# A hybrid-attention decoder layer: expert gathers in slots of 128 tokens, one PSUM copy of the tokens for the dot products, and deeper gather rings

## The reference, cut to what matters

```python
q = (xc @ w_pq).reshape(c, 8, 2, 128)                       # 8 heads, two half-queries
s = jnp.einsum('chpd,hpkd->chpk', q, sub_keys)
sv, si = lax.top_k(s, 16)                                   # best 16 keys of each half
cand = (sv[:, :, 0, :, None] + sv[:, :, 1, None, :]).reshape(c, 8, -1)
cid = (si[:, :, 0, :, None] * 128 + si[:, :, 1, None, :]).reshape(c, 8, -1)
cv, ci = lax.top_k(cand, 16)                                # 16 experts a head: 128 a token
eid = jnp.take_along_axis(cid, ci, axis=-1)
gate = jax.nn.softmax(cv, axis=-1)
act = jax.nn.gelu(jnp.einsum('chkd,cd->chk', u_emb[eid], xc), approximate=False)
out = jnp.einsum('chk,chkd->cd', gate * act, v_emb[eid])    # 1024 floats of u and of v an expert
```

## Time and profile before

| | |
|---|---|
| median of three timed runs | 1012.64 us (1012.56 to 1013.12) |
| span of the profiled execution | 1080.4 us |
| DMA moved in the span | 381.54 MB, mean 353 GB/s |
| of it POOL's queue (gathers) / SP's queue | 304.81 MB / 75.78 MB |
| busy: PE / DVE / ACT / POOL | 69% / 64% / 37% / 58% |
| gathers issued by POOL | 576 |

### The profile page before, as it was taken

The page is one execution under the profiler, slowest core; times in us unless marked ns, Lnnn a source line. Parts: engine busy times, 40 slices in busy tenths (PEclk is TensorE's granted clock), DMA queues, the critical chain, the costliest instruction groups (busy, mean ns, idle before and its releaser), DMA issues.

```text
span 1080.4 us, 13828 instructions
## 1 busy us (share of the span) xinstructions
PE 742.8 (69%) x4217; PEld 379.1 (35%) x4217; DVE 686.7 (64%) x1725; ACT 404.0 (37%) x1154; POOL 622.1 (58%) x584
## 2 busy tenths in 40 slices
PE   8999986554798677766536768757637567765444
PEld 3575834111354435543212233323213235231111
DVE  1363776997288543698695559988974535639542
ACT  1162142332356470333223346354516742322412
POOL 0000275777667765475565656766775665667664
PEclk9999997877778899988867878877778878887656
DMA  9924699999979999999899999999998999999997
GB/s 364 331 79 184 217 349 411 411 360 377 336 252 359 348 400 412 398 379 379 278 314 325 373 388 353 391 362 362 407 412 308 411 417 416 414 411 409 382 376 270
DMA packets 122443, 381.54 MB, mean 353 GB/s; under 512 B 16026, under 2 KB 40682, under 8 KB 117122
## 3 DMA queue, kind: packets, MB, share of 16 engines
q0 software_dynamic: 83696, 304.81, 74.0%
q1 hardware_dynamic: 38578, 75.78, 19.2%
q10 hardware_dynamic: 96, 0.07, 0.0%
HBM read 378.16 MB, written 4.14 MB: 354 GB/s over the span
## 4 chain that ended last, share of the span: by engine, by line
PE 28%; DVE 19%; issue 17%; ACT 10%; another core or an unknown queue 9%; DMA 8%; POOL 6%; SPq 3%; ACTq 0%; POOLq 0%; DVEq 0%
PE bank L463 17%; PE acc L463 9%; DVE rows L1453 6%; DMA w_uq_sb<-in_w_uq 3%; PE bank L466 3%; POOL rows L1978 3%; DMA rows<-in_peer_v,eid 2%; POOL rows L1996 2%; ACT spread L1101 2%; ACT L1092 1%; SPq L2069 1%; DVE shared L1793 1%; DVE shared L1782 1%; ACT shared L1063 1%
## 5 line engine op out<-in xcount | busy, mean ns | idle before, releaser
L463 PE MATMUL acc<-rows,spread 128*64 128x512 f32 (+1 forms) x1124 | 329.3, 682 | 143.9 <-ACT spread L1101 51.9
L1978 POOL DMA_INDIRECT rows<-in_peer_v,eid x254 | 275.8, 1086 | 160.5 <-issue 66.6
L1996 POOL DMA_INDIRECT rows<-in_peer_u,eid x184 | 193.2, 1050 | 109.0 <-issue 54.7
L463 PEld LDWEIGHTS acc<-rows,spread 128*64 128x64 f32 (+1 forms) x1124 | 89.1, 156 | 310.3 <-issue 240.2
L1453 DVE CUSTOM_DVE_ANT_0 rows<-rows,xr_even 128x1024 f32<-128x1024 f32 x89 | 108.1, 1218 | 34.0 <-DMA rows<-in_peer_u,eid 26.4
L1453 DVE CUSTOM_DVE_ANT_0 rows<-rows,xr_odd 128x1024 f32<-128x1024 f32 x95 | 116.2, 1223 | 19.6 <-DMA rows<-in_peer_u,eid 18.8
L1101 ACT ACTIVATE spread<-wide_consts,wts 128x64 f32<-128x64 f32 (+1 forms) x288 | 83.7, 337 | 35.2 <-remote 25.0
L1996 POOL DMA_INDIRECT first_u<-in_peer_u,eid x37 | 38.2, 1032 | 101.5 <-DVE eid L1835 81.6
L463 PE MATMUL acc<-more_v,spread 128*64 128x512 f32 (+1 forms) x140 | 73.6, 695 | 18.9 <-ACT spread L1101 9.9
L1094 ACT ACTIVATE wts<-gelus,gate 128x1 f32<-128x1 f32 x288 | 69.1, 287 | 4.7
L1063 ACT ACTIVATE shared<-bank 128x512 f32<-128x512 f32 (+4 forms) x68 | 27.8, 456 | 76.3 <-remote 35.5
(11 more groups left out here) (278 smaller groups left out, 1222.4 us busy)
## 6 DMA issues: line engine op xcount, KB each, us to landing
wring<-in_w_pq SPq DMA_DIRECT2D x12, 1024.0 KB
z<-in_w_pq SPq DMA_DIRECT2D x5, 1024.0 KB, 4.8
wring<-in_cache_ckv SPq DMA_DIRECT2D x40, 128.0 KB
rows<-in_w_in SPq DMA_DIRECT2D x2, 2048.0 KB, 15.2
rows<-in_w_pq SPq DMA_DIRECT2D x2, 2048.0 KB, 8.3
wring<-in_w_out SPq DMA_DIRECT2D x4, 1024.0 KB
wring<-in_cache_kv SPq DMA_DIRECT2D x32, 128.0 KB
rows<-in_peer_v,eid POOLq DMA_INDIRECT x254, 7.5
```

The costliest lines, as they stand in the source:

```text
L463: return T.matmul(o, lhsT=l, rhs=r, start=start, stop=stop, skip_group_check=True)
L1978: nc.gpsimd.indirect_dma_start(out=v_ring[V_PLACE[n]], out_offset=None, in_=inp["peer_v"], in_offset=bass.IndirectOffsetOnAxis(ap=eid[t][: ...
L1996: nc.gpsimd.indirect_dma_start(out=u_ring[U_PLACE[n]], out_offset=None, in_=inp["peer_u"], in_offset=bass.IndirectOffsetOnAxis(ap=eid[t][: ...
```

## The change

- A u slot of tiles 0 and 1 holds one expert of all 128 tokens; a v slot still holds two experts of 64 tokens. So one copy of the tokens serves all dots: `xr_odd` is gone, and `xr` is one 128x1024 tensor in PSUM. For tile 0 the norm writes it directly; for tile 1 one copy fills it, for tile 2 four of 32 partitions as before.
- There are two tables of row numbers: `eid` for u (one instruction a part in place of four) and `eid_v` for v (the four as before, counted by a new semaphore, `v_slots_ready`, for which POOL waits ahead of the first v gather of each part).
- The dots of a u pair are (token, expert) and the weights of a v pair (expert and token half). ACT turns one into the other: it makes `wts` with four 64-partition multiplications a pair, two of which read one half of the partitions and write the other.
- The SBUF that POOL's DMA descriptors take is set to 4096 bytes a partition (`SCRATCH`; the default is 16384). With this and `xr_odd`, two more u buffers and two more v buffers fit: RU 9, RV 11. The first four u gathers and three v gathers no longer go to `rows`.
- The wait for `z1_stored` moves from DVE (ahead of its first copy) to POOL (ahead of v slot 2).

```diff
-RU, RV, RD = 7, 9, 4
+RU, RV, RD = 9, 11, 4
+SCRATCH = 4096
...
-RC = 8 * PAIR
+RC = 12 * PAIR
...
+                first = n - BASE[t] - PAIR + 1
                 for i in range(PAIR):
-                    g = A.activation(wts[:, k + i:k + i + 1], gelus[:, k + i:k + i + 1], ACT.Copy,
-                                     scale=gate[t][:, n - BASE[t] - PAIR + 1 + i:n - BASE[t] - PAIR + 2 + i])
+                    for j in range(PAIR if t < 2 else 0):
+                        src, dst = slice(WIDE * j, WIDE * j + WIDE), slice(WIDE * i, WIDE * i + WIDE)
+                        g = A.activation(wts[dst, k + j:k + j + 1], gelus[src, k + i:k + i + 1], ACT.Copy,
+                                         scale=gate[t][src, first + i:first + i + 1])
...
-                V.tensor_tensor_reduce(out=u, in0=u, in1=xr[j], scale=1.0, scalar=0.0,
+                V.tensor_tensor_reduce(out=u, in0=u, in1=xr, scale=1.0, scalar=0.0,
...
-                for j, q in SPREAD[t]:
-                    i = V.scalar_tensor_tensor(out=laid(t, p, j, q, eid[t]), in0=picked(t, p, j, q, ea), scalar=float(KEYS),
-                                               in1=picked(t, p, j, q, eb), op0=ALU.mult, op1=ALU.add)
-                i.then_inc(slots_ready, 1)
+                V.scalar_tensor_tensor(out=eid[t][:, ks], in0=ea[:, ks], scalar=float(KEYS), in1=eb[:, ks],
+                                       op0=ALU.mult, op1=ALU.add).then_inc(slots_ready, 1)
+                for j, q in HALVES if t < 2 else []:
+                    i = V.scalar_tensor_tensor(out=laid(p, j, q, eid_v[t], t), in0=picked(p, j, q, ea, t), scalar=float(KEYS),
+                                               in1=picked(p, j, q, eb, t), op0=ALU.mult, op1=ALU.add)
+                if t < 2:
+                    i.then_inc(v_slots_ready, 1)
...
-                if n == 4:
+                if t < 2 and n - BASE[t] in STARTS[t]:
+                    pool.wait_ge(v_slots_ready, CHOSEN[t] + STARTS[t].index(n - BASE[t]) + 1)
+                if n == 2:
+                    pool.wait_ge(z1_out, 16)
+                if n == 6:
                     z1_done.wait(pool, 2)
...
-                    if n in (2, 6):
-                        ready(pool, ("pq", {2: 1, 6: 2}[n], 0))
+                    if n in (4, 8):
+                        ready(pool, ("pq", {4: 1, 8: 2}[n], 0))
...
-    nc = bacc.Bacc("TRN2", target_bir_lowering=False, num_devices=1)
+    nc = bacc.Bacc("TRN2", target_bir_lowering=False, num_devices=1, dynamic_dma_scratch_size=SCRATCH)
```

More of the change, by code:

```diff
@@ L137, in build @@
         bias_d = sb("bias_d", [128, NH, 256])
-        more_u = sb("more_u", [128, DM])
+        more_u = [sb(f"more_u{i}", [128, DM]) for i in range(3)]
         x_b = [sb(f"x{i}", [128, DM]) for i in range(2)]
         x = [x_b[t % 2] for t in range(3)]
[L142 to L145, removed]
+        more_v = [sb(f"more_v{i}", [128, DM]) for i in range(3)]
+        eid = [sb(f"eid{t}", [128, SLOTS[t]], U32) for t in range(2)]
+        eid.append(eid[0][:, 0:SLOTS[2]])
+        eid_v = [sb(f"eid_v{t}", [128, SLOTS[t]], U32) for t in range(2)] + [eid[2]]
+        gate = [sb(f"gate{t}", [128, SLOTS[t]]) for t in range(2)]
+        gate.append(gate[0][:, 0:SLOTS[2]])
         ckv_nat = sb("ckv_nat", [128, 3, KVL])
@@ L155, in build @@
         rows_f = rows[:, :, :].rearrange("p a b -> p (a b)")
-        u_ring = [first_u[:, :], more_u[:, :]] + [rows[:, i, :] for i in range(5)] + [b[:, :] for b in x_b]
-        v_ring = [more_v[:, :]] + [rows[:, i, :] for i in (5, 6, 7, 8, 9, 10, 11, 12)]
+        u_ring = [first_u[:, :], *(b[:, :] for b in more_u)] + [rows[:, i, :] for i in range(5)] + [b[:, :] for b in x_b]
+        v_ring = [b[:, :] for b in more_v] + [rows[:, i, :] for i in (5, 6, 7, 8, 9, 10, 11, 12)]
         v_ring += [u_ring[p] for p in V_END.values()]
@@ L267, in build @@
         zs = [z, z, bias_df[0:32, 0:DIN]]
-        z1_kept = xr_odd[:, 0:512]
-        loose = [first_u[:, :], more_u[:, :], more_v[:, :], g_fin[:, :]]
+        z1_kept = more_v[2][:, 0:512]
+        loose = [first_u[:, :], more_u[0][:, :], more_v[0][:, :], g_fin[:, :]]
         z2_kept = [f[:, :, :].rearrange("p a b -> p (a b)") for f in spread]
@@ L280, in build @@
         acc = ctx.enter_context(nc.psum_tensor("acc", [128, DM], F32))
-        xr_even = ctx.enter_context(nc.psum_tensor("xr_even", [128, DM], F32))
-        xr = [xr_even[:, :], xr_odd[:, :]]
+        xr_bank = ctx.enter_context(nc.psum_tensor("xr", [128, DM], F32))
+        xr = xr_bank[:, :]
         banks = [ctx.enter_context(nc.psum_tensor(f"bank{i}", [128, 512], F32)) for i in range(NRING)]
@@ L378, in build @@
         gate_exp = sem("gate_exp")
-        slots_ready = sem("slots_ready")
+        slots_ready, v_slots_ready = sem("slots_ready"), sem("v_slots_ready")
         chain_v, chain_a = sem("vector_chain"), sem("scalar_chain")
@@ L1448, in dot_slot, with replicate @@
             def dot_slot(t, n):
-                k, j = n % RC, n % PAIR if t < 2 else 0
+                k = n % RC
                 u = u_ring[U_PLACE[n]]
                 dve.wait_ge(u_in[U_PLACE[n]], (U_USE[n] + 1) * 16)
-                V.tensor_tensor_reduce(out=u, in0=u, in1=xr[j], scale=1.0, scalar=0.0,
+                V.tensor_tensor_reduce(out=u, in0=u, in1=xr, scale=1.0, scalar=0.0,
                                        op0=ALU.mult, op1=ALU.add, accum_out=dots[:, k:k + 1]).then_inc(dots_done, 1)
[L1456 to L1463, removed]
+            def replicate(t):
+                dve.wait_ge(dots_done, BASE[t])
+                m = P[t]
+                for q in range(128 // m):
+                    i = V.tensor_copy(xr[m * q:m * q + m, :], xn2[0:m, :])
                 link(V, i)
@@ L1941, in _ @@
                     experts.rest(t - 1)
-                    replicate(t, range(PAIR if t < 2 else 1))
+                    replicate(t)
                     experts.rest(t, 6)
```

35 lines of the change are left out of this document (16 added, 19 removed).

## The result

The changed kernel takes 1017.47 us (median of 20; 1015.80 to 1018.97), the kernel before 1014.37. The ratio is 1.0036 with an interval of 1.0028 to 1.0045: slower, by 3.6 us of 1014, where 979 us had been forecast.

What follows compares the result with a forecast made beforehand. The prediction took an unsteady gather stream as the bound, paced by POOL or the DMA engines, with no single owner. Terms -29 - 10 - 4 - 1 + 8 = -36 us gave 1044.4, times 0.937 = 979 us; range 943 to 1000.

Steps and rivals of the forecast that it cites:

- The base: Whole kernel: terms summed on the profiled 1080.4 us span, then scaled by 0.937 to timed runs, giving 979 us.
- the lock: POOL's gathers beside dots reading `xr_odd` from SBUF: reading PSUM shortens them, 29 us gained, bounds 0 to 57.2.
- the rings: u and v buffers: two more of each cut POOL's waits, 10 us gained, bounds 0 to 29.6.
- the 96 us of lost rate: Nine windows from 119 us on: a steady 413 GB/s would take 845 us instead of 941.
- The pace of POOL: Gather stream: where gathers are long, POOL issues one every 1.38 us, against 1.27 the DMA engines need.
- Start: First u gathers: more stand ahead of POOL's two waits for PE, 4 us gained, bounds 2.5 to 5.4.
- Copies on DVE: DVE: twelve copies into `xr` become five, with fewer instructions for `eid` and gates; 1 us gained, bounds 0 to 5.
- Descriptor memory: POOL's DMA descriptors: 4 KB instead of 16 KB holds more gathers than the buffers do, taken at 0 us.
- ACT: Pairs of tiles 0 and 1: two more multiplications each, 61 us more busy; 8 us lost, bounds 0 and 61.
- The consumers set the pace: Rival, whole stream: POOL's gain turns into waits for dots and sums; 1001 to 1011 us, chance 0.12.
- ACT on the path: Slower rival, tiles 0 and 1: all 128 pairs pay 0.48 us before each sum; 1028 us, chance 0.08.
- the small descriptor memory: Slower rival, gather stream: POOL waits for descriptor room, holding 339 GB/s; +88 us, some 1095 us, chance 0.03.

Runs made afterwards that it cites:

- first profile: The profiled execution of the kernel before, unchanged, on which the prediction rests: span 1080.4 us, against a timed median of 1012.64 us.
- second profile: The kernel before, unchanged, profiled once more: span 1011.5 us.
- b_psum: The kernel before with every dot reading xr_even in PSUM, the xr_odd copy made but not read: 1011.50 us, ratio 0.9983.
- a_r79: The changed kernel with RU cut from 9 to 7 and RV from 11 to 9: 1017.66 us, ratio to before 1.0045.
- b_ring: The kernel before with RU raised from 7 to 9, RV from 9 to 10, and 4 KB of descriptor memory: 1012.07 us, ratio 0.9990.
- a_pad_r79: The changed kernel with 32 empty bytes a partition ahead of wring and RU 7, RV 9: 1019.23 us, ratio to before 1.0048.
- b_scr4: The kernel before with only the descriptor memory set to 4096 bytes a partition: 1013.73 us, ratio 1.0006.
- a_act2: The changed kernel with two weight multiplications a pair on all 128 partitions instead of four: 1017.68 us, ratio to before 1.0041.
- a_w256: The changed kernel with wring, z, ql_t and shared back on a multiple of 256 bytes, gelus and wts shortened: 1007.56 us, ratio to before 0.9942.
- b_off: The kernel before with 32 empty bytes a partition ahead of wring, nothing else changed: 1025.32 us, ratio 1.0109.
- a_all256: The changed kernel with wring, z, ql_t and also the gathers' places on a multiple of 256 bytes: 993.61 us, ratio to before 0.9795.

## Why the prediction was wrong, point by point

**The base.** The first step that failed is "The timed median is 0.937 of the profiled span (1012.64 / 1080.4), so 1044.4 x 0.937". It scales a disturbed execution as if every part of it were 6.7% too long. It was not: the time lay in the dips to 339 to 388 GB/s, the very time that the lock and the rings were to win back. By the prediction's own measure, length x (1 - rate/413), the windows from 160 to 880 lose 81 us in the first profile and 18 in the second, which runs there at 394 to 412 GB/s. So most of the 96 us of lost rate were not the kernel's. The prediction named its own sign of being wrong, a time above 1000 with POOL's gathers short, and that is what came.

**The pace of POOL.** "about 1.38 us from one to the next: longer than the 1.27 that the DMA engines need" left out SP's queue, 75.78 MB of the 381.54. What a gather has is the stretch by the count: 576 in some 871 us (first issue at 116.40, last at 986.89 in the second profile), 1.51 us. POOL at 1.36 keeps up with that in the mean, and falls short only where SP brings little, as in 260:400 (5.5 of 55.3 MB, at 395 GB/s).

**The terms.** *Lock*, 29 us forecast: 1.7 (b_psum). The lower bound was named with its reason, "a POOL that issues earlier may just wait longer for a buffer"; that is what happened. *Rings*, 10: 0.9 to 1.5 (a_r79, b_ring, a_pad_r79), of some 5 us won at 400:530 and 3.5 lost at the end, a loss that the sum had no term for. *Start*, 4, bounds 2.5 to 5.4: 5.9; right in kind, a little over its bound. The first wait was 3.96 and not 3.4 (5.92 - 2 x 1.24), and 0.60 was left of the second. *Copies on DVE*, 1: not tried alone; the first gather came at 115.98 us instead of 116.40, but two runs that leave DVE's start as it was have it at 115.54 (b_psum) and 115.56 (b_scr4), so no gain is shown. *Descriptor memory*, 0: 0 (b_scr4, and with deeper rings b_ring). *ACT*, 8 lost: 0 (a_act2). ACT's busy time grew by 86.6 us and not 61, as the 64-partition multiplication takes longer than the plain one: four of them 1.21 us, where two took 0.48.

```profile
304.29 1.21 ACT L1100 ACTIVATE wts<-gelus,gate 64x1 f32<-64x1 f32 x4
305.53 0.59 ACT L1110 ACTIVATE spread<-wide_consts,wts 128x64 f32<-128x64 f32 x2
```

Part of it did reach PE, whose wait for the spread is 54.0 us against 22.8 in a_act2; it cost nothing in the end, as PE would else have waited for data.

**The missing term.** `RC = 8 * PAIR` to `12 * PAIR` is a line of the diff that the prediction passed over. It makes three small tensors 32 bytes longer each and moves wring, z and ql_t off their multiple of 256: 9.5 us (a_w256 against the changed kernel, by the ratios). By the single runs the sum is -1.7 - 1.0 - 5.9 + 9.5 = +0.9 us; measured are +3.6. The 2.7 us between are not closed by a run, and the single intervals are 1 to 2 us to each side. Two findings bear on them: the lock and the rings fill the same window (260:400 has 408 GB/s with the lock gone, 401 with the rings deeper and 408 with both), and the end takes 20.1 us against 16.2.

**The rivals.** None of them was it. ACT on the path and the small descriptor memory, the two slower cases, are excluded by a_act2 and b_scr4. "The consumers set the pace" had the right outcome for the lock and the rings, but the pace is set by the DMA engines. The change, without its accident, is worth 5.9 us (a_w256, ratio 0.9942), as much as the start alone.

## What to carry to other kernels

Before a profile is costed, lay its span beside the timed runs: where it is several per cent longer, look for stalls without a releaser and take another profile, since lost time that is only in that execution can't be won back. Where DMA share is 1.0 in every window, price a change by bytes, by when the stream starts, by what a packet takes, and by how the stream ends; a stall of an engine beside it turns into a wait. And when a diff changes the size of any tensor, print where every later DMA target starts before and after.

## What the runs showed of the hardware

That 32 bytes of empty SBUF cost a kernel 11 us (b_off, 1.0109) was not expected, nor that gathers slow down without being moved: POOL's went from 162 to 168 ns a packet though they landed where they had before, and what had moved, beside operands of the engines, were targets of SP's queue. Starts of all large DMA targets on a multiple of 256 bytes brought 409 to 418 GB/s in the windows of gathers (a_all256), and 14.0 us more than wring, z and ql_t alone (1007.56 to 993.61). Which of the targets in the second step matter most was not tried. Deeper rings made the stream end more slowly: the last 5 MB took 20.1 us with rings of 9 and 11 (after) and 16.5 with 7 and 9 (a_r79); with every target on a multiple of 256 the deep rings took 15.4 (a_all256).
